# Layer norm statistics of three projection stages of a hybrid decoder layer, centred about the mean of four blocks and summed among the products; the first two weight chunks of each FFN multiplied together

## The reference

```python
def layer_norm(x, g, b):
    mu = jnp.mean(xf, -1, keepdims=True)
    var = jnp.mean(jnp.square(xf - mu), -1, keepdims=True)
    y = (xf - mu) * lax.rsqrt(var + LN_EPS)
    return y * g + b

h = x * (1.0 + sc1) + sh1
x = layer_norm(ALPHA * x + 0.5 * g1 * swiglu(h, f1_in, f1_out), ln_g[0], ln_b[0])
h = x * (1.0 + sc2) + sh2
mixed, state = mixer(h)                  # w_qkv, two attention mixers with caches
x = layer_norm(ALPHA * x + g2 * (mixed @ w_o), ln_g[1], ln_b[1])
h = x * (1.0 + sc3) + sh3
x = layer_norm(ALPHA * x + 0.5 * g3 * swiglu(h, f2_in, f2_out), ln_g[2], ln_b[2])
```

## Time and profile before

| what | us |
|---|---|
| device time, median of 3 runs | 1725.79 |
| lowest and highest run | 1721.04, 1736.04 |
| span of the profiled execution, first to last instruction | 1722.1 |
| busy: TensorE, VectorE, ScalarE, GpSimd | 1523.3, 659.6, 511.7, 66.3 |

### The profile page before, as it was taken

The page is one execution under the profiler, slowest core; times in us unless marked ns, Lnnn a source line. Parts: engine busy times, 40 slices in busy tenths (PEclk is TensorE's granted clock), DMA queues, the critical chain, the costliest instruction groups (busy, mean ns, idle before and its releaser), DMA issues.

```text
span 1722.1 us, 31526 instructions
## 1 busy us (share of the span) xinstructions
PE 1523.3 (88%) x12377; PEld 1338.7 (78%) x12377; DVE 659.6 (38%) x1293; ACT 511.7 (30%) x829; POOL 66.3 (4%) x156
## 2 busy tenths in 40 slices
PE   4899999989996999788888777778789999989996
PEld 2788999989985767655565555548689999989995
DVE  1222323222235524255555555545542323222224
ACT  2322222211114222234444444442242222221113
POOL 0100000000002000000000000000010000000000
PEclk9899999999998999999999999988889999999998
DMA  9993222222212232379889998772112222232211
GB/s 337 385 310 117 86 75 84 85 84 84 84 53 69 61 129 70 119 215 275 264 265 275 269 251 263 236 215 78 50 49 86 85 74 85 85 91 68 84 50 55
DMA packets 212310, 245.52 MB, mean 143 GB/s; under 512 B 8511, under 2 KB 152377, under 8 KB 209154
## 3 DMA queue, kind: packets, MB, share of 16 engines
q1 hardware_dynamic: 212226, 244.42, 46.7%
HBM read 237.31 MB, written 7.08 MB: 142 GB/s over the span
## 4 chain that ended last, share of the span: by engine, by line
PE 77%; DVE 6%; DMA 5%; SPq 5%; issue 3%; ACT 3%; ACTq 0%; DVEq 0%
PE ps L273 53%; PE ps L769 10%; DMA kv<-in_cache_diff_k_dram 3%; SPq L975 2%; PE ps L1111 2%; PE ps L1058 2%; SPq L955 2%; PE ps L1070 2%; PE ps L558 2%; PE ps L381 2%; PE ps L1154 2%; DMA wada<-in_w_ada_dram 1%; DVE PP L1287 1%; PE ps L1129 1%; DVE KC L1279 1%
## 5 line engine op out<-in xcount | busy, mean ns | idle before, releaser
L252 ACT ACTIVATE whi<-w 128x1024 fp32r<-128x1024 f32 (+1 forms) x152 | 171.1, 1129 | 801.4 <-PE ps L273 687.1
L258 DVE TENSOR_TENSOR wlo<-w,whi 128x1024 fp32r<-128x1024 f32 (+1 forms) x152 | 200.0, 1318 | 412.3 <-ACT whi L252 411.9
L273 PE MATMUL ps<-hhi,whi 128*128 128x288 f32 x1536 | 332.9, 298 | 19.0 <-DVE hlo L311 13.6
L273 PE MATMUL ps<-hlo,whi 128*128 128x288 f32 x1536 | 330.7, 297 | 0.0
L273 PE MATMUL ps<-hhi,wlo 128*128 128x288 f32 x1536 | 330.2, 297 | 0.0
L273 PEld LDWEIGHTS ps<-hhi,whi 128*128 128x128 f32 x1536 | 249.1, 190 | 26.3 <-DVE hlo L311 14.0
L273 PEld LDWEIGHTS ps<-hlo,whi 128*128 128x128 f32 x1536 | 249.5, 190 | 0.0
L273 PEld LDWEIGHTS ps<-hhi,wlo 128*128 128x128 f32 x1536 | 249.2, 190 | 0.0
L273 PE MATMUL ps<-ffhi,whi 128*128 128x288 f32 x704 | 152.8, 299 | 9.2 <-DVE wlo L258 9.2
L1058 PEld LDWEIGHTS ps<-ident,kv 128*128 128x128 f32 (+1 forms) x896 | 98.6, 146 | 77.5 <-issue 59.1
L1058 PE MATMUL ps<-ident,kv 128*128 128x128 f32 (+1 forms) x896 | 122.4, 278 | 35.3 <-DMA kv<-in_cache_diff_k_dram 19.1
(11 more groups left out here) (158 smaller groups left out, 1585.0 us busy)
## 6 DMA issues: line engine op xcount, KB each, us to landing
w<-in_ffn_w_in_dram SPq DMA_DIRECT2D x88, 512.0 KB, 3.9
wada<-in_w_ada_dram SPq DMA_DIRECT2D x18, 2048.0 KB, 12.4
kv<-in_cache_diff_k_dram SPq DMA_DIRECT2D x128, 256.0 KB, 5.1
kv<-in_cache_diff_v_dram SPq DMA_DIRECT2D x128, 256.0 KB, 3.6
w<-in_ffn_w_out_dram SPq DMA_DIRECT2D x32, 704.0 KB, 4.6
w<-in_w_qkv_dram SPq DMA_DIRECT2D x24, 512.0 KB, 3.7
kv<-in_cache_win_k_dram SPq DMA_DIRECT2D x16, 768.0 KB, 6.1
kv<-in_cache_win_v_dram SPq DMA_DIRECT2D x16, 768.0 KB, 9.0
```

The source lines that it names most:

```text
L252: nc.scalar.activation(whi[:, slot, 0:w], w32[:, slot, 0:w], ACT.Copy).then_inc(ph.hi, 1)
L258: nc.vector.tensor_tensor(wlo[:, slot, 0:w], w32[:, slot, 0:w], whi[:, slot, 0:w].bitcast(F32), ALU.subtract).then_inc(ph.lo, 1)
L273: m = pe.matmul(ps[:, banks + h, 0:TH], w, x[:, kk, h * TH:(h + 1) * TH], start=(kk == 0 and n == 0), stop=(kk == kall - 1 and n == 2))
```

## The change

In each projection stage, a mean of the first four blocks (twice the sum of four over 1024 is their mean over 512 features) is taken in block 4's products (`shift`), and all blocks have it subtracted, blocks 4 to 7 before their residual is added, 0 to 3 after. ScalarE squares the shifted blocks as they are done (into `sqh`, laid over `hhi`/`hlo`, or `sqf`, over `ffhi`), and TensorE sums the squares column-tiled into four quarters of 144 tokens (`TQ`), six blocks (st 1: four) among the last products and the others behind them. The variance is then the mean of the squares less the square of the remaining mean, on 144 columns, one quarter in each group of 32 partitions; root and reciprocal run on 144 columns, and `sel` spreads the result to all partitions by matmuls. `project_tensor` is written out without a hardware loop. A root of one element at the start of `project_scalar` loads ScalarE's function table there. The FFN's first pair of chunks is multiplied block by block, the second half of the tokens two blocks behind the first, and both `used` signals come at the end of the pair; both halves of the third modulation vector's products stand ahead of it.

```diff
-            pe.wait_ge(sem("step_acc"), (st + 1) * (DB - 1))
-            for h in range(2):
-                m = pe.matmul(ps[:, 4 + h, 0:TH], one_d[:], tmp[:, 3, h * TH:(h + 1) * TH], start=True, stop=True)
-            m.then_inc(sem("step_mean"), 1)
-            for d in range(DB):
-                pe.wait_ge(sem("step_sq"), st * DB + d + 1)
-                for h in range(2):
-                    m = pe.matmul(ps[:, 6 + h, 0:TH], one_d[:], tmp[:, d % 3, h * TH:(h + 1) * TH],
-                                  start=(d == 0), stop=(d == DB - 1))
-                m.then_inc(sem("step_var"), 1)
...
+            def shift():
+                pe.wait_ge(sem("step_acc"), st * (DB - 1) + 3)
+                pe.matmul(ps[:, 6, 0:NPR], one_h[:], tmp[:, 3, 0:NPR], start=True, stop=True)
+                pe.matmul(ps[:, 4, 0:NSM], one_h[:], tmp[:, 3, NPR:T], start=True, stop=True).then_inc(sem("step_s"), 1)
+            def variance(d):
+                pe.wait_ge(sem("step_sq"), st * DB + d + 1)
+                for j in range(4):
+                    r, c = quarter(j)
+                    m = pe.matmul(ps[r, 5, 0:TQ], one_d[:, 0:32], squares(st)[:, d, c], start=(d == 0), stop=(d == DB - 1),
+                                  tile_position=(0, 32 * j))
+                m.then_inc(sem("step_var"), 1)
...
+            for d in range(DB):
...
+                    chunk_products(ph, slot, nk_chunk, xhi, xlo, hh * nk_chunk, kall, 2 * (d % 2), halves if d == 0 else None,
+                                   (5, shift) if n_half == 1 and d == 4 else None)
+                    if n_half == 2 and hh == 0 and d == 4:
+                        shift()
+                    if n_half == 2 and hh == 0 and d == 7:
+                        for v in range(6):
+                            variance(v)
+                if n_half == 1 and d == 6:
+                    for v in range(4):
+                        variance(v)
+            for v in range(6 if n_half == 2 else 4, DB - 1):
+                variance(v)
...
+            mean_quarters(tmp[:, 3, :], True)
+            mean_samples(tmp[:, 3, :], True)
+            mean_wide(tmp[:, 3, :], True)
+            pe.wait_ge(sem("step_res"), (st + 1) * DB)
+            mean_quarters(xT[:, DB - 1, :], False)
+            mean_samples(xT[:, DB - 1, :], False).then_inc(sem("step_mq"), 1)
+            mean_wide(xT[:, DB - 1, :], False).then_inc(sem("step_mean"), 1)
+            variance(DB - 1)
+            pe.wait_ge(sem("step_rs"), st + 1)
+            for j in range(3):
+                pe.matmul(ps[:, 7, j * TQ:(j + 1) * TQ], sel[:, j, :], tmp[:, 1, 0:TQ], start=True, stop=True)
...
 project_vector
+                if d == DB - 1 and after:
+                    split_lo(after, 0, 0)
+                if d == 4:
+                    eng.wait_ge(sem("step_s"), st + 1)
+                    for later in range(4, DB):
+                        shift(later)
+                    shift_samples(4)
...
+            eng.tensor_tensor(tmp[:, 0, TQ:2 * TQ], ps[:, 5, 0:TQ], tmp[:, 0, 0:TQ], ALU.subtract).then_inc(sem("step_vv"), 1)
+            centre(st, 0)
             eng.wait_ge(sem("step_std"), st + 1)
-            eng.reciprocal(tmp[:, 3, :], tmp[:, 3, :]).then_inc(sem("step_rs"), 1)
+            eng.reciprocal(tmp[:, 1, 0:TQ], tmp[:, 0, 2 * TQ:3 * TQ]).then_inc(sem("step_rs"), 1)
+            centre_samples(st)
+            for d in range(1, DB if st == 2 else CENTRED):
+                centre(st, d)
...
 modulate_vector
             for d in range(DB):
-                if d + 1 < DB:
-                    normalise(d + 1)
+                if st > 0 and d + 1 < DB:
+                    if d + 1 >= CENTRED:
+                        centre(st - 1, d + 1)
+                    normalise(st - 1, d + 1)
...
 project_scalar
+            eng.activation(stat[:, 60:61], stat[:, 5:6], ACT.Sqrt)
...
 ffn_in_tensor
-            pe.wait_ge(sem("step_slo"), st + 1)
+            def first_pair():
+                if ffn == 0:
+                    ada_products(MODS_AHEAD, 0)
+                    ada_products(MODS_AHEAD, 1)
+                for k in range(DB + 2):
+                    for gu in range(2):
+                        if k == 0:
+                            pe.wait_ge(ph.lo, ph.base + gu + 1)
+                        if k < DB:
+                            pe.wait_ge(sem("step_hlo"), st * DB + k + 1)
+                            block_products(ph, gu, k, hhi, hlo, k, DB, 2 * gu, 0)
+                    for gu in range(2):
+                        if k >= 2:
+                            if k == 2:
+                                pe.wait_ge(sem("step_slo"), st + 1)
+                            m = block_products(ph, gu, k - 2, hhi, hlo, k - 2, DB, 2 * gu, 1)
+                            if k == DB + 1:
+                                m.then_inc(ph.used, 1)
...
 qkv_tensor
-            pe.wait_ge(sem("step_slo"), 2)
...
+                            if g == 0 and c == 0 and t == PT_:
+                                pe.wait_ge(sem("step_slo"), 2)
```

More of the change, by code:

```diff
@@ L259, in split_lo, with block_products, chunk_products @@
                                     ALU.subtract).then_inc(ph.lo, 1)
-        def chunk_products(ph, slot, nk, xhi, xlo, k0, kall, banks, halves=None):
+        def block_products(ph, slot, k, xhi, xlo, kk, kall, banks, h):
+            m = None
+            wh = whi[:, slot, k * P:(k + 1) * P]
+            wl = wlo[:, slot, k * P:(k + 1) * P]
+            for n, (w, x) in enumerate(((wh, xhi), (wh, xlo), (wl, xhi))):
+                m = nc.tensor.matmul(ps[:, banks + h, 0:TH], w, x[:, kk, h * TH:(h + 1) * TH],
+                                     start=(kk == 0 and n == 0), stop=(kk == kall - 1 and n == 2))
+            return m
+        def chunk_products(ph, slot, nk, xhi, xlo, k0, kall, banks, halves=None, middle=None):
             pe = nc.tensor
@@ new lines, in variance, with mean_quarters @@
+            def variance(d):
[5 more added lines that the diff above has]
+                m.then_inc(sem("step_var"), 1)
+            def mean_quarters(x, first):
+                for j in range(4):
+                    r, c = quarter(j)
+                    m = pe.matmul(ps[r, 4, 0:TQ], one_d[:, 0:32], x[:, c], start=first, stop=not first,
+                                  tile_position=(0, 32 * j), skip_group_check=True)
+                return m
@@ L385, in project_vector @@
+            pe.matmul(ps[:, 7, 3 * TQ:NPR], sel[:, 3, :], tmp[:, 1, 0:NPR - 3 * TQ], start=True, stop=True)
+            pe.matmul(ps[:, 5, TQ:TQ + NSM], sel[:, 3, :], tmp[:, 1, NPR - 3 * TQ:TQ], start=True,
+                      stop=True).then_inc(sem("step_bc"), 1)
+        CENTRED = 3
         def project_vector(st, ph, n_half, i_gate, after):
@@ new lines, in square @@
+            def square(d):
+                eng.wait_ge(sem("step_sub"), 10 * st + 10)
+                eng.wait_ge(sem("step_res"), st * DB + d + 1)
+                eng.activation(squares(st)[:, d, :], xT[:, d, :], ACT.Square).then_inc(sem("step_sq"), 1)
+            eng.activation(stat[:, 60:61], stat[:, 5:6], ACT.Sqrt)
+            for c in range(0 if n_half == 2 else 2, n):
+                split_hi(ph, c, c % 2)
+                if n_half == 2 and c >= 11:
+                    for d in {11: (0, 1), 12: (2, 3), 13: (4,), 14: (), 15: (5,)}[c]:
+                        square(d)
+                if n_half == 1 and c == 7:
+                    for d in range(5):
+                        square(d)
@@ L441, in project_scalar @@
             if after:
                 split_hi(after, 0, 0)
+            for d in (6,) if n_half == 2 else (5, 6):
+                square(d)
+            if after:
                 split_hi(after, 1, 1)
-            for d in range(DB):
-                eng.wait_ge(sem("step_cen"), st * DB + d + 1)
-                if d >= 3:
-                    eng.wait_ge(sem("step_var"), st * DB + d - 2)
-                eng.activation(tmp[:, d % 3, :], xT[:, d, :], ACT.Square).then_inc(sem("step_sq"), 1)
@@ L614, in start_pool @@
             eng.memset(stat[:, 5:6], LN_EPS).then_inc(sem("pool_set"), 1)
+            eng.memset(one_h[:], 2.0 / D).then_inc(sem("pool_set"), 1)
+            eng.memset(sel[:], 0.0).then_inc(sem("pool_set"), 1)
+            eng.wait_ge(sem("pool_set"), 6)
+            for j in range(4):
+                eng.memset(sel[32 * j:32 * j + 1, j, :], 1.0).then_inc(sem("pool_set"), 1)
+            eng.wait_ge(sem("pool_set"), 10)
         def start_tensor():
```

113 lines of the change are left out of this document (81 added, 32 removed).

## The result

| | kernel before | changed kernel |
|---|---|---|
| median, us | 1728.28 (4 runs, 1721.04 to 1736.04) | 1699.47 (4 runs, 1696.01 to 1703.41) |
| span of the profiled execution | 1722.1 | 1694.2 |

The ratio is 0.9848, 95% interval 0.9821 to 0.9875: faster by 1.5%, 28.8 us between the medians and 27.9 between the spans. Forecast were 28.6 off both.

A forecast was written before the change was run, and what follows sets the result against it. TensorE, 77% of the chain, was taken as the bound. Net terms for stages 0, 1, 2 and the start, -10.4, -9.9, -4.8 and -3.5, sum to -28.6 us: 1725.8 to 1697.2 us, range 1685 to 1715.

The forecast's parts named there:

- The three tails: Last projection product to TensorE's next phase, stages 0, 1 and 2: shorter by 14.9, 12.3 and 9.3 us.
- the quarters ran side by side: Rival: column-tiled variance and mean quarters run one after the other, 0.97 us a set; 1715.8 us, chance 0.08.
- nothing was lost downstream: Rival: attention's transfers don't follow TensorE, so stage 0's 10.4 us is lost; 1707.6 us, chance 0.06.
- their code isn't fetched too slowly: Rival: TensorE's 2496 straight-line products are fetched too slowly; 1759.6 us at 25 ns each, chance 0.03.
- Tail 0: Stage 0, behind the last product: first normalise at 7.5 us, TensorE restarting at 13.1 instead of 27.97, -14.9.
- the 0.9 us of gain that I had set beside the sum: Normalise reading PSUM avoids GpSimd contention: at most 0.9 us more gain in each of stages 0 and 1.
- Tail 1: Stage 1's tail and FFN 3's first pair: third chunk at 31.8 us instead of 44.1, -12.3.
- The start: FFN 1's first pair: reordered modulation products and block-by-block start bring the third chunk earlier, -3.5 us, bounds 0 and -5.7.
- that case: At the start, the modulation weights' second half landing at 50: gain 2.4 us, against 4.7 if by 46.
- Hand-overs: FFN to projection, stages 0 and 2: the one-element root and its table load add 1.4 us each.
- Products: Shift and variance sets among the projection products add 3.1, 2.4 and 3.1 us of TensorE in stages 0, 1, 2.
- my range: Whole kernel: 1685 us with all terms at their better bound, to 1715 towards the serial quarters.

The follow-up runs named there:

- experiment 3: Changed kernel without the one-element root at the start of each projection: 1697.64 us, ratio 0.9797.
- experiment 4: Changed kernel with TensorE waiting for `step_slo` ahead of all QKV products, as before the change: 1698.52 us, one run.
- experiment 1: Changed kernel with the first FFN pair back in its old chunk-by-chunk order behind `step_slo`: 1706.12 us, ratio 0.9849.
- experiment 2: Kernel before with only the first FFN pair changed to block by block: 1727.35 us, ratio 0.9997.
- experiment 10: Changed kernel with added matmuls whose results nobody reads, in the tails and before the hand-overs: 1700.09 us, ratio 0.9847.
- experiment 5: Changed kernel with no variance set among the products, all seven behind the last product: 1700.82 us, one run.
- experiment 6: Changed kernel with the first pair's gate chunk ended first and SiLU's table loaded early: 1700.93 us, ratio 0.9864.
- experiment 8: Changed kernel with the reciprocal ahead of centring block 0 and the last variance ahead of the full-width mean: 1700.33 us, one run.
- experiment 11: Changed kernel with gate chunk first, SiLU's table early, swapped tail order and the one-element root behind the fifteenth split: 1689.29 us, ratio 0.9792.
- experiment 12: The kernel of experiment 11 with the added matmuls of experiment 10: 1690.23 us, ratio 0.9779.

## Why the prediction was right, and where it wasn't

**The mechanism** held: every tail is shorter because the squares don't wait for the mean and the small steps run on 144 columns. The three tails sum to -34.6 where -36.5 was forecast. No rival took place: the quarters ran side by side (0.27 a set, not 0.97); nothing was lost downstream, since QKV's last product ends 7.0 us earlier (714.34 for 721.37), which is what the start and stage 0 gained less QKV's 2.6; and the 2496 written-out products of the projections follow each other every 0.133 us as before, or every 0.130 (228 and 233 of them in 30 us above), so their code isn't fetched too slowly.

**Tail 0**, normalise at 7.5, measured 8.4: TensorE's own part, put at 3.34, took 3.99 (514.81 to 518.80), and `sel`, for which a spread between full and half clock was left, ran at half nearly throughout: 1.61 + 0.35 + 0.41 = 2.37. Where it ran at full clock (experiments 3 and 4) the normalise came at 7.7. From the normalise to the first product 5.6 was taken, 5.45 measured. Of it the timelines show, VectorE first, then GpSimd beside it:

```profile
524.41 0.68 DVE L327 TENSOR_TENSOR xT<-xT,ps 128x512 f32<-128x512 f32 x1
525.01 1.26 DVE L349 SCALAR_TENSOR_TENSOR tmp<-xT,modT,hhi 128x512 f32<-128x512 f32 x1
...
526.79 0.97 DVE L349 SCALAR_TENSOR_TENSOR tmp<-xT,modT,hhi 128x512 f32<-128x512 f32 x1
```

```profile
524.64 1.08 POOL L393 TENSOR_TENSOR tmp<-xT,modT 128x512 f32<-128x512 f32 x1 [336.69 <-DVE xT L332]
525.80 1.41 POOL L395 TENSOR_TENSOR tmp<-tmp,modT 128x512 f32<-128x512 f32 x1
```

The normalise (L327), one input in PSUM, keeps its 0.68 beside GpSimd; L349, both tiles in SBUF, takes 1.26 and then 0.97 for the 0.74 that it takes later. By the Trainium skill, "SBUF — State Buffer", section "Who interferes with whom", only the second should contend, and the trace agrees, with those numbers. VectorE's instructions lose 0.52 + 0.23 = 0.75 us beside GpSimd here, where they lost 1.7 before: the 0.9 us of gain that I had set beside the sum.

**Tail 1**: the forecast of 31.8 was right within 0.6, but its reason was only half right. I credited the block-by-block pair together with the tail. Experiments 1 and 2 show the pair worth 0.2 and 1.0 us there: it starts 5.2 (3.9) us earlier, spends part of that at half clock, and the late `used` signals open a pause of 2.77. That pause I had forecast (2.8), but I had not priced the old order behind the new tail.

**The start** is the term that failed: -3.5 forecast, -1.0 in the profile and in experiment 2. The weights' second half landed at 49.5, and the chain then reads:

```profile
35.58 13.93 DMA wada<-in_w_ada_dram
...
49.56 3.64 PE ps L714 x32
53.20 12.68 PE ps L272 x93
```

My own steps, with the landing at 50 in place of 46, give an end 4 us later, 66.5, and the third chunk at 69.3: -0.8. The -2.4 that I wrote for that case was a slip, and the value taken lay between it and the -4.7 of the earlier landing.

**Hand-overs**: +1.5 each for +1.4. The Trainium skill, "ScalarE: Activation LUTs", section "What ACT_TABLE_LOAD costs", adds a drain of 1.38 us to the load. The trace disagrees: the root starts 0.01 after the load's 1.28 is over (363.64 and 364.93), and both hand-overs grew by 1.5, so the measurement decides. What I had not asked is whether the load was on the path where it stood: experiment 3 shows it hidden there, so the edit costs 3.0 us and gains none.

**Products**: shift and six sets cost 1.03 + 1.61 = 2.64 of the 3.1 forecast, the set at 0.27 for 0.35. The rest of projection 0's +4.0 is half clock: 2.6 us more of it cost 1.3. Projection 2's 0 has two causes: 2.1 us less half clock gave back 1.05, and the pace of 0.130 us a product in its first half some 1.8 (8 chunks of 66 products, 0.0033 us each). That is luck, and no part of the change. QKV's +2.6 was not in my sum: TensorE comes out of the tail and QKV has 9.5 us at half clock where it had 3.8; experiment 10 ties the part behind the tail to the pause. The windows of the pause and of the twelve microseconds behind it, in the changed kernel:

```profile
523.00:529.00 6.00, 0.51 (x2) 0.37 (x2) 5.76 (x9) 3.78 (x5) 2.49 (x2) 0.50 0.14 60
529.00:535.00 6.00, 6.00 (x16) 4.62 (x16) 5.90 (x11) 4.69 (x7) 0.00 (x0) 0.52 0.01 3
535.00:541.00 6.00, 6.00 (x28) 4.64 (x27) 4.00 (x7) 4.65 (x7) 1.57 (x2) 1.00 0.00 0
```

The granted clock had fallen to 0.50 at 521.1 already, among `sel`'s matmuls. After 5.5 us without a matmul the first six of QKV get 0.52 and hold 16 matmuls, the next six 1.00 and 28.

**The total** came within a microsecond or two because the start (2.5 short), the tails (1.9 short) and QKV (2.6) were offset by attention's -4.8 and by projection 2's clock and pace (2.8). Without attention's share the spans differ by 23.1; between medians of four runs each, in which such chances average out in part, the changed kernel lies 28.8 under the kernel before, and its near twins (experiments 1, 5, 6 and 8; 5 and 8 ran once) 21 to 27 under theirs. The lower end of my range, 1685, was not summed rightly: the better bounds that I named for it give 8 to 9 us more, not 12.

## What to carry to other kernels

Statistics that must follow the last block can be taken about a mean that is known early, and then only a correction stands behind it; that gained 1.5%, and where the sums were placed among the products mattered nothing, since the engine that does them is the bound. A table load or a signal has a price only where it stands on the path: before moving one, look whether it was hidden, and whether its new place lies in that engine's idle time (experiment 11, which moves it there, with a `used` signal given earlier, SiLU's table loaded earlier and the order of 8, had a median 10 us lower, 9.5 by its stretches). Starting an engine earlier on partial input gains only if what follows the whole is ready earlier too.

## What was unexpected in the hardware

Four column-tiled float32 matmuls of 144 columns take 0.27 us in all, where four of the same form one after the other at full width would have cost about 0.97 by the earlier trace rows, and going from full matmuls to tiles and back costs about 0.1 (504.15 to 505.76 for six sets). The time that TensorE stays at 0.50 behind a pause varies between executions of like code: QKV had 3.1 to 11.4 us of it over the profiles in which nothing filled the pause. Filling the pauses removed it there in experiment 10 (1.00 in the window that had 0.81), and still did not lower the median in either of two kernels: in experiment 12 a remaining pause of 1.89 us was followed by 3.4 us of it in QKV, where 1.30 in experiment 10 was followed by none. And the same products at the same granted clock followed each other every 0.133 us in most profiles and every 0.130 in some stretches of four; for that no run here has the cause.
